# A hybrid decoder step on one core: the 64x64 inversions composed from 16x16 blocks by a block-nilpotent Horner scheme

## What is computed

```python
L = jnp.where(strict, jnp.einsum('nbhcd,nbhsd->nbhcs', k_beta, kb) * decay, 0.0)
eye = jnp.eye(C, dtype=L.dtype)                      # C = 64
tinv = lax.linalg.triangular_solve(eye + L, jnp.broadcast_to(eye, L.shape),
                                   left_side=True, lower=True, unit_diagonal=True)
u = jnp.einsum('nbhcs,nbhse->nbhce', tinv, v_beta)
w = jnp.einsum('nbhcs,nbhsd->nbhcd', tinv, k_beta * jnp.exp(gc)[..., None])
```

## Time and profile before

| | |
|---|---|
| median of three runs | 2028.67 us (2026.51 to 2037.93) |
| span of the profiled execution | 2031.9 us |
| TensorE matmuls busy | 1902.7 us, 94% |
| TensorE weight loads busy | 1734.3 us, 85% |
| VectorE busy | 1255.8 us, 62% |
| ScalarE busy | 938.5 us, 46% |
| mean granted TensorE clock | 0.960 |

### The profile page before, as it was taken

How to read it: one execution, slowest core, us unless ns; L and a number is a source line. 1 busy time by engine, 2 the same in 40 slices (tenths; PEclk the granted TensorE clock), 3 DMA queues, 4 the chain that set the end, 5 groups by cost and what they waited for, 6 DMA issues and landing times.

```text
span 2031.9 us, 45422 instructions
## 1 busy us (share of the span) xinstructions
PE 1902.7 (94%) x19380; PEld 1734.3 (85%) x19380; DVE 1255.8 (62%) x2186; ACT 938.5 (46%) x1834; POOL 77.3 (4%) x158
## 2 busy tenths in 40 slices
PE   5999989989999988889999999899899999889998
PEld 4899978888888777788989999788899788679997
DVE  3545356765446765778556654578654585769953
ACT  3334455544456534423444444645443664353343
POOL 0000000110000100000000000001200011000000
PEclk8999999988999998999999999999899999899999
DMA  8877755555465565699775666545543445269873
GB/s 256 239 225 219 209 164 167 164 148 150 138 167 156 151 157 136 186 269 279 208 203 156 178 178 186 166 135 156 135 122 102 135 120 147 69 160 259 252 201 108
DMA packets 556519, 353.38 MB, mean 174 GB/s; under 512 B 19620, under 2 KB 515270, under 8 KB 555022
## 3 DMA queue, kind: packets, MB, share of 16 engines
q1 hardware_dynamic: 490634, 302.74, 52.3%
q10 hardware_dynamic: 60756, 38.81, 7.2%
q0 software_dynamic: 4928, 8.92, 1.8%
HBM read 332.27 MB, written 18.50 MB: 173 GB/s over the span
## 4 chain that ended last, share of the span: by engine, by line
PE 75%; DVE 10%; DMA 6%; ACT 5%; issue 3%; POOL 1%; SPq 0%; ACTq 0%; DVEq 0%; POOLq 0%
PE bank L926 72%; DMA ring<-in_w_ada 2%; DMA ring<-in_ffn_up 2%; DVE ring_r L744 2%; PE bank L657 1%; DVE far L1999 1%; DMA far<-t_blocks 1%; ACT w_hi_r L736 1%; PE bank L670 1%; POOL far L638 1%; DVE y L1999 1%; DVE big L1999 1%; DVE h L2002 1%; PE bank L665 1%; DMA far<-in_state_gdn_ssm 1%
## 5 line engine op out<-in xcount | busy, mean ns | idle before, releaser
L926 PE MATMUL bank<-big_r,w_hi_r 128*128 128x264 f32 x4160 | 1077.7, 293 | 47.5 <-DVE h_r L2002 25.6
L926 PE MATMUL bank<-big_r,ring_r 128*128 128x264 f32 (+1 forms) x3456 | 994.2, 288 | 0.0
L926 PEld LDWEIGHTS bank<-big_r,w_hi_r 128*128 128x128 f32 x4160 | 748.2, 191 | 109.3 <-issue 86.2
L926 PE MATMUL bank<-h_r,w_hi_r 128*128 128x264 f32 x2752 | 797.1, 290 | 0.0
L744 DVE TENSOR_TENSOR ring_r<-ring,w_hi_r 128x1024 fp32r<-128x1024 f32 (+2 forms) x440 | 523.6, 1195 | 391.3 <-ACT w_hi_r L736 387.3
L926 PEld LDWEIGHTS bank<-big_r,ring_r 128*128 128x128 f32 (+1 forms) x3456 | 662.8, 192 | 1.0
L736 ACT CAST w_hi_r<-ring 128x1024 fp32r<-128x1024 f32 (+2 forms) x440 | 452.0, 1028 | 449.0 <-PE bank L926 201.2
L926 PEld LDWEIGHTS bank<-h_r,w_hi_r 128*128 128x128 f32 x2752 | 530.4, 193 | 1.7 <-issue 0.5
L926 PE MATMUL bank<-ring,c 128*32 128x256 f32 x1152 | 94.5, 409 | 17.0 <-DMA ring<-in_w_ada 14.1
L926 PE MATMUL bank<-big,far 64*64 64x64 f32 (+2 forms) x1440 | 101.8, 251 | 0.0
L926 PEld LDWEIGHTS bank<-big,far 64*64 64x64 f32 (+1 forms) x1440 | 85.1, 137 | 9.2 <-issue 8.8
(11 more groups left out here) (304 smaller groups left out, 1946.1 us busy)
## 6 DMA issues: line engine op xcount, KB each, us to landing
ring<-in_ffn_up SPq DMA_DIRECT2D x176, 512.0 KB, 4.9
ring<-in_w_in SPq DMA_DIRECT2D x148, 512.0 KB, 3.7
ring<-in_w_ada SPq DMA_DIRECT2D x144, 512.0 KB, 4.4
ring<-in_ffn_down SPq DMA_DIRECT2D x64, 512.0 KB, 4.5
far<-in_state_gdn_ssm ACTq DMA_DIRECT2D x28, 512.0 KB, 6.3
ring<-in_ffn_down SPq DMA_DIRECT2D x32, 384.0 KB, 3.5
ring<-in_w_out SPq DMA_DIRECT2D x16, 512.0 KB, 4.7
out_sample_gdn_ssm<-far ACTq DMA_DIRECT2D x16, 512.0 KB, 5.5
```

The source lines that it names most:

```text
L926: return pe.matmul(out, lhsT, rhs, start=start, stop=stop)
```

## The change

The 64x64 inverse is composed in another way. With D the block diagonal of 16x16 blocks, X the negated product of the inverse of D with what lies below the block diagonal (in the transposed layout of the kernel), X is block-nilpotent: its fourth power is zero. The inverse is then a Horner scheme in X applied to the inverse of D: each of three steps multiplies by X and adds the inverse of D.

- Step 0 makes X: one product of 32 matmuls, now with 48 columns, in two banks. VectorE masks it with `below`, in two operations of 128x384.
- Step 1: X by the last 48 columns; VectorE adds in two operations of 128x384. Step 2: X by the last 32 columns; one addition of 128x512. Step 3: X by the last 16 columns; one addition of 128x256, straight into the result. Only the transposed inverse is carried, its partner is no longer updated.
- So a run has four products, with 48, 48, 32 and 16 columns, where it had five with 32. Step 1 no longer has its second product. Steps stay in the same turns, and each still waits for VectorE's result of the step before.
- `settled` copies two pieces, 128x256 and 128x512, where it copied one of 128x512. `clear` zeroes 16 columns of each unit in `x_b` where it zeroed 64 (128x256 for 128x1024).
- The setup builds one mask `below` (one select on GpSimd) in place of two masks in `level` (four selects); the row factors `upper` and their three VectorE operations go.

```diff
-        level = sb("level", 2, 32)
-        upper = sb("upper", 2)
+        below = sb("below", 48)
...
-        def level_cols(v, n, side):
-            return v.rearrange("p u (a h t) -> p u a h t", h=2, t=1 << n)[:, :, :, side, :]
-
-        def unit_cols(v, n, side):
-            return v.rearrange("p (a h t) -> p a h t", h=2, t=1 << n)[:, :, side, :]
-
-        def level_bank(bank, n):
-            return banks[bank][:, :].rearrange("p (u a t) -> p u a t", u=UNITS, t=1 << n)
-
-        def pair_cols(both, n, w, side, u=None):
-
-            cols = "p u (a h t) -> p u a h t" if n == 4 else "p u (h a t) -> p u a h t"
-            v = both[:, :, :, w].rearrange(cols, h=2, t=B16)[:, :, :, side, :]
+        def columns(both, w, first, u=None):
+
+            v = both[:, :, first:C, w]
             return v if u is None else v[:, u]
 
-        INV_PE = 5
-
-        def inv_count(run, s):
-            return INV_PE * run + (1, 2, 4, 5)[s]
+        def half_bank(bank):
+            return banks[bank][:, 0:UNITS // 2 * 48].rearrange("p (u t) -> p u t", t=48)
+
+        def whole_bank(bank, n):
+            return banks[bank][:, 0:UNITS * n].rearrange("p (u t) -> p u t", t=n)
 
...
-                i = act.mul(x_b, bm(ident64[:, :], UNITS), 0.0)
+                i = act.mul(x_b[:, :, 48:C], bm(ident64[:, 0:B16], UNITS), 0.0)
...
-            elif s == 2:
-                pe.wait_ge(inv_t.sem, inv_t.at(2 * run + 1))
-            if s % 2 == 0:
-                for u in range(UNITS):
-                    for hf in HALVES:
-                        i = pe.matmul(banks[2][hf, u * 32:(u + 1) * 32].rearrange("p (a t) -> p a t", t=B16), lt[hf, u, :],
-                                      pair_cols(both[hf], n, 0, 0, u), start=True, stop=True)
-                i.then_inc(inv_pe.sem, inv_pe.one())
-                return
-            pe.wait_ge(inv_x.sem, inv_x.at(2 * run + s // 2 + 1))
-            if n < 5:
-                for u in range(UNITS):
-                    for hf in HALVES:
-                        i = pe.matmul(banks[4][hf, u * 32:(u + 1) * 32].rearrange("p (a t) -> p a t", t=1 << n), both[hf, u, :, 1],
-                                      unit_cols(x_b[hf, u, :], n, 0), start=True, stop=True)
-                i.then_inc(inv_pe.sem, inv_pe.one())
+            else:
+                pe.wait_ge(inv_x.sem, inv_x.at(3 * run + s))
             for u in range(UNITS):
                 for hf in HALVES:
-                    i = pe.matmul(banks[3][hf, u * 32:(u + 1) * 32].rearrange("p (a t) -> p a t", t=B16), x_b[hf, u, :],
-                                  pair_cols(both[hf], n, 1, 1, u), start=True, stop=True)
+                    if s < 2:
+                        out = banks[2 + u // 8][hf, u % 8 * 48:(u % 8 + 1) * 48]
+                        moving = columns(both[hf], 1, B16, u) if s else both[hf, u, 0:48, 0]
+                    else:
+                        n = (32, 16)[s - 2]
+                        out, moving = banks[s][hf, u * n:(u + 1) * n], columns(both[hf], 0, C - n, u)
+                    i = pe.matmul(out, x_b[hf, u, :] if s else lt[hf, u, :], moving, start=True, stop=True)
             i.then_inc(inv_pe.sem, inv_pe.one())
 
         def settled(act, run):
 
             lt, both, x_b = inv_sets[run]
-            act.wait_ge(inv_t.sem, inv_t.at(2 * run + 1))
-            act.wait_ge(inv_x.sem, inv_x.at(2 * run + 2))
-            act.copy(lt[:, :, 0:32].rearrange("p u (a t) -> p u a t", t=B16), pair_cols(both, 5, 1, 0)).then_inc(inv_c.sem, inv_c.one())
+            act.wait_ge(inv_x.sem, inv_x.at(3 * run + 3))
+            act.copy(lt[:, :, 0:B16], both[:, :, 0:B16, 1])
+            act.copy(lt[:, :, B16:48], both[:, :, B16:48, 0]).then_inc(inv_c.sem, inv_c.one())
 
         def invert_dve(dve, run, s):
 
             lt, both, x_b = inv_sets[run]
-            n = 4 + s // 2
-            dve.wait_ge(inv_pe.sem, inv_pe.at(inv_count(run, s)))
-            if s % 2 == 0:
-                by = level[:, n - 4, :].rearrange("p (a t) -> p a t", t=1 << n).unsqueeze(1).to_broadcast([P, UNITS, 32 >> n, 1 << n])
-                dve.tensor_tensor(level_cols(x_b, n, 0), level_bank(2, n), by, ALU.mult).then_inc(inv_x.sem, inv_x.one())
-                dve.wait_ge(inv_x.sem, inv_x.all())
+            dve.wait_ge(inv_pe.sem, inv_pe.at(4 * run + s + 1))
+            if s == 3:
+                dve.tensor_tensor(lt[:, :, 48:C], columns(both, 1, 48), whole_bank(3, B16), ALU.add).then_inc(inv_t.sem, inv_t.one())
+                dve.wait_ge(inv_t.sem, inv_t.all())
                 return
-            if n < 5:
-                t_0 = pair_cols(both, n, 0, 0)
-                dve.tensor_tensor(t_0, t_0, level_bank(4, n), ALU.add)
-                dve.wait_ge(inv_pe.sem, inv_pe.at(inv_count(run, s) + 1))
-            tt_1 = pair_cols(both, n, 1, 1)
-            into = lt[:, :, 32:64].rearrange("p u (a t) -> p u a t", t=B16) if n == 5 else tt_1
-            dve.scalar_tensor_tensor(into, level_bank(3, 4), upper[:, n - 4:n - 3], tt_1, ALU.mult, ALU.add).then_inc(inv_t.sem, inv_t.one())
-            dve.wait_ge(inv_t.sem, inv_t.all())
+            if s == 2:
+                i = dve.tensor_tensor(columns(both, 0, 32), columns(both, 1, 32), whole_bank(2, 32), ALU.add)
+            for g in range(2 if s < 2 else 0):
+                us = slice(UNITS // 2 * g, UNITS // 2 * (g + 1))
+                if s == 0:
+                    i = dve.tensor_tensor(x_b[:, us, 0:48], half_bank(2 + g), bm(below[:, :], UNITS // 2), ALU.mult)
+                else:
+                    i = dve.tensor_tensor(both[:, us, B16:C, 0], both[:, us, B16:C, 1], half_bank(2 + g), ALU.add)
+            i.then_inc(inv_x.sem, inv_x.one())
+            dve.wait_ge(inv_x.sem, inv_x.all())
...
-                for n in range(2):
-                    b = 16 << n
-                    v = level[0:64, n, :].rearrange("p (a t) -> p a t", t=b)
-                    select(v, [[-2 * b, 32 // b], [0, b]], -b, 1, ALU.is_ge, 0.0)
-                    select(v, [[2 * b, 32 // b], [0, b]], 2 * b - 1, -1, ALU.is_ge, 0.0)
-                pool.memset(level[64:128, 0, 0:1], -1.0).then_inc(pool_done.sem, pool_done.one())
+                select(below[0:64, :].rearrange("p (a t) -> p a t", t=B16), [[-B16, 3], [0, B16]], -B16, 1, ALU.is_ge, 0.0)
+                pool.memset(below[64:128, 0:1], -1.0).then_inc(pool_done.sem, pool_done.one())
...
-                                pe.wait_ge(inv_t.sem, inv_t.at(4))
+                                pe.wait_ge(inv_t.sem, inv_t.at(2))
...
-                    pe.wait_ge(inv_t.sem, inv_t.at(6))
+                    pe.wait_ge(inv_t.sem, inv_t.at(3))
...
-                        dve.tensor_reduce(upper[:, :], level[:, :, :], AX_X, ALU.add).then_inc(dve_chain.sem, dve_chain.one())
-                        dve.wait_ge(dve_chain.sem, dve_chain.all())
-                        for n in range(2):
-                            i = dve.tensor_scalar(upper[:, n:n + 1], upper[:, n:n + 1], 0.5 ** (4 + n), 1.0, ALU.mult, ALU.add)
-                        i.then_inc(dve_chain.sem, dve_chain.one())
-                        dve.wait_ge(dve_chain.sem, dve_chain.all())
```

More of the change, by code:

```diff
@@ L775, in _ @@
                 pool.memset(mean_all[:, :], 1.0 / D).then_inc(pool_done.sem, pool_done.one())
-                for buf, value in ((ones_all[:, :], 1.0), (ones_half[:, :], 0.0), (masks[:, :, :], 1.0), (level[:, :, :], -1.0)):
+                for buf, value in ((ones_all[:, :], 1.0), (ones_half[:, :], 0.0), (masks[:, :, :], 1.0), (below[:, :], -1.0)):
                     pool.memset(buf, value).then_inc(pool_chain.sem, pool_chain.one())
@@ L1590, in _ @@
                         act.dma_start(masks[64:128, :, :], masks[0:64, :, :]).then_inc(g2_in.sem, g2_in.one())
-                        act.dma_start(level[64:128, :, :], level[0:64, :, :]).then_inc(g2_in.sem, g2_in.one())
+                        act.dma_start(below[64:128, :], below[0:64, :]).then_inc(g2_in.sem, g2_in.one())
                         act.wait_ge(edge_tr.sem, edge_tr.nth(2))
@@ L1870, in _ @@
                                 if run == 1:
-                                    act.wait_ge(inv_t.sem, inv_t.at(2))
+                                    act.wait_ge(inv_t.sem, inv_t.at(1))
                                     act.wait_ge(inv_c.sem, inv_c.at(1))
@@ L1883, in see_state @@
                         act.dma_start(gs_seen[n % 5], sample_state(I["state_gdn_ssm"][l], n)).then_inc(gs_in[n // 2 % 3].sem, gs_in[n // 2 % 3].one())
-                    act.wait_ge(inv_t.sem, inv_t.at(6))
+                    act.wait_ge(inv_t.sem, inv_t.at(3))
                     act.wait_ge(s_pe.sem, s_pe.at(3))
```

## The result

The changed kernel takes 2009.4 us, the median of four runs (2004.23 to 2015.53), against 2033.3 us for the kernel before in the same comparison (2026.51 to 2038.3). The ratio is 0.989 with a 95% interval of 0.9855 to 0.9924, so it is faster by 15 to 29 us, most likely 22. A second set with an unchanged copy gave 0.9875 (0.9843 to 0.9906). The forecast was 2015.8 us and -12.9 us: the sign and the main term held, the size came out too small. The 2009.4 us lie 0.4 us inside the prediction's wide range (2009 to 2022.5) and outside its own (2012 to 2019.5). Part of that is luck: both were worked out from a before of 2028.67 us, and beside after it took 2033.3. The change itself, -22 us, is more than the wide range allowed (2028.67 - 2009 = 19.7 us).

What follows compares the result with a forecast made beforehand. TensorE's instruction stream was taken as the bound, the inversion a small part of it. Terms 11.25 + 0.5 + 0.3 + 0.8 = 12.9 us, from 2028.67 to 2015.8 us; own range 2012 to 2019.5, for 8 in 10 2009 to 2022.5.

Steps and rivals of the forecast that it cites:

- main term: TensorE: one product of 1.94 us fewer in each of six inversion runs, 11.6 us saved.
- wide range: Span of times given 8 chances in 10, reaching into the rivals: 2009 to 2022.5 us.
- The products: TensorE, inversion: weight loads set a product's time, 48 or 16 columns cost as 32; 11.25 us saved after 0.35 given back.
- VectorE in layer 1, run 0: TensorE's wait for VectorE before step 3 grows from 0.31 to about 0.7 us, giving back 0.35 us.
- Rival E: VectorE's queue in run 0 of both layers doesn't move up, losing the removed product there: 9.0 us gain, 2019.7 us; chance 0.12.
- The price of a half-clock stretch: TensorE behind run 0 of layer 0: 10 us at 0.50 costs 4.3 us.
- The clear: ScalarE's clear before run 0 is 0.64 us shorter, TensorE's wait 0.6 us shorter; 0.4 us a layer, 0.8 us.
- Step 3 to run 1: VectorE's lighter step 3 shortens TensorE's wait before run 1 by 0.34 us a layer; counted 0.25 each, 0.5 us.
- rival D: Fewer half-clock stretches, as behind layer 1's run 1: 2.6 us more gain, 5 with part of a second, 2011 us; chance 0.18.
- the prediction's own sign for the clock: Wrong by the clock if stretches at 0.50 after the runs change in number by two or more.
- C: Rival: more half-clock stretches behind TensorE's waits, five of them making it 8.6 us slower, 2037 us; chance 0.05.

Runs made afterwards that it cites:

- e9: Kernel before without step 1's second product and VectorE's addition of it, so its composed inverse lacks that part; 2020.02 us, 0.9928 of before.
- e1: Changed kernel with a fifth product of 32 columns put back in step 1 of each run, its result unread; 2019.76 us, 0.9936 of before.
- e3: Changed kernel with 6 and 4 dense matmuls on constants ahead of TensorE's waits for blocks in runs 0 and 1; 2015.02 us, 0.9903 of before.
- e7: Changed kernel with both the edits of e3 and e4; 2004.58 us, 0.987 of before.
- e6: Changed kernel with the clear of x_b in runs 0 and 2 over all 64 columns again; 2014.12 us, 0.9903 of before.
- e2: Changed kernel with steps 2 and 3 also at 48 columns, the extra ones overwritten, same number of matmuls; 2012.85 us, 0.9897 of before.
- e4: Changed kernel with VectorE's solve of run 1's blocks one turn later; 2010.36 us, 0.9908 of before.
- e5: Changed kernel with that solve, runs 0 and 1 and the clear of run 1 one turn later; 2011.51 us, 0.9897 of before.

## Why the prediction was right, and where it wasn't

**The products: right.** The step "6 x 1.94 = 11.6 us" is what the runs show: 384 records fewer, 2.00 and 1.98 us a product, 13.7 us gained by removing it alone (e9, at the same clock), 11.8 us lost by putting it back (e1). Measured alike, 48 columns cost 0.01 us more than 32 (2.00 for 1.99), inside the stated bound of 0.1 for each. The 67.9 us that the prediction says the old products hold are durations of overlapping records; thirty products at 1.94 us are 58.

**VectorE in layer 1, run 0: the mechanism right, the size wrong.** I expected a wait of about 0.7 us before step 3. The trace has 3.01 us before step 2 and 0.77 before step 3. TensorE's timeline in layer 1, then VectorE's, then the chain of waits:

```profile
1433.78 2.07 PE L652 MATMUL bank<-far 64*64 64x48 f32 x64 [3.23 <-DMA far<-t_blocks]
...
1439.79 1.74 PE L652 MATMUL bank<-far 64*64 64x48 f32 x54
...
1447.65 2.21 PE L652 MATMUL bank<-far 64*64 64x32 f32 x64 [3.01 <-DVE far L677]
...
1455.08 2.04 PE L652 MATMUL bank<-far 64*64 64x16 f32 x64 [0.77 <-DVE far L671]
```

```profile
1440.70 0.38 DVE L602 TENSOR_SCALAR big<-big 128x256 f32<-128x256 f32 x1 [3.78 <-DMA big<-lt_blocks]
...
1446.58 1.01 DVE L677 TENSOR_TENSOR far<-far,bank 128x384 f32<-128x384 f32 x2
...
1457.64 0.41 DVE L667 TENSOR_TENSOR far<-far,bank 128x256 f32<-128x256 f32 x1
```

```profile
1436.52 4.06 DMA big<-lt_blocks
...
1446.66 0.94 DVE far L677 x2
...
1458.09 1.93 ACT far L617
1460.30 3.91 POOL far L628 x7
1464.21 4.57 DMA far<-t_blocks
1468.82 2.80 PE bank L652 x64
```

The order is: VectorE stands 3.78 us at 1440.70 before the fetched blocks of run 1, solves them, and only then adds step 1 of run 0, although TensorE was done with that product at about 1439.79 + 1.74 = 1441.53. Behind it are run 0's last step, the clear of run 1, its scatter and its first product. This chain from a fetch to the products of run 1 runs beside TensorE's dense work, and what TensorE gains ahead of its end becomes idle time later. That the solve in this place is the cause is shown by e3 and e7, which differ by the solve's turn alone and both have the full clock in run 0: 7.0 us of these waits with the solve here, none with it a turn later. Nor are the new operations on VectorE the cause: e9, with the old ones, waited 1.89 and 0.76 us at the same two places, also at full clock. Here the clock had not fallen behind run 0's wait:

```profile
440.00:449.00 9.00, 8.92 (x88) 8.83 (x89) 4.27 (x17) 1.24 (x2) 0.57 (x1) 0.50 0.19 47
...
1434.00:1440.00 6.00, 6.00 (x114) 5.39 (x112) 1.02 (x2) 0.78 (x3) 0.57 (x1) 1.00 0.52 139
```

These two windows of after are run 0 of layer 0 and of layer 1, at 0.50 and 1.00. From 1440 to 1457 us of before, TensorE gained 4.2 us in layer 1, the missing product and a stretch that had been at half clock; by 1465 us it had given 5.2 back, 3.8 of them in the two waits and the rest in a stretch at 0.50 behind the first (1449.6 to 1452.6 us). So over run 0 it was 1.0 us behind where it had been. In the copy, whose run 0 stood at half clock in layer 1 as before's did, 3.0 us were gained by 1457 and 1.4 given back, so 1.7 us were left. Rival E had the mechanism and the place right, then: in after the product's time was lost there, together with a half-clock stretch's. How much is lost differs between executions of the same code. e3 confirms it from the other side.

**The price of a half-clock stretch: too high.** The step "4.3 us for 10 us at 0.50" is the price on TensorE alone. Over the executions it is 0.34 us for one, not 0.43. In run 0 most of it is hidden under the chain above: from run 0's first product to that of run 1, after needs 35.5 us in layer 0 at half clock and the copy 34.1 at full, but in layer 1 after needs 35.0 at full and the copy 33.8 at half. Behind layer 0's loop it is full (4.3 us for 10.2).

**The clear: wrong in what follows from it.** TensorE's wait before run 0 was to be 0.6 us shorter than 2.98; it is 3.43 us in after, 3.12 in the copy, and its product started at 440.08 where it had started at 440.15. The clear itself did shrink as forecast, from 1.07 to 0.43 us, and the scatter behind it started sooner. What took the gain back is the landing of the last block. These are the chain of waits in before, then in after:

```profile
435.88 4.22 DMA far<-t_blocks
```

```profile
430.32 0.43 ACT far L619
...
434.94 5.09 DMA far<-t_blocks
```

The prediction carried the 0.64 us straight through to TensorE's start; the landing varies by more than that from one place to the next (5.32 us in layer 1 of before, where TensorE waited 4.08 us; 3.23 in after). In layer 1 e9, with the long clear, waited 3.15 us, as short as after. So no run shows a wait that the clear made shorter, and the effect on the time (e6) stays unplaced.

**Step 3 to run 1: not contradicted.** TensorE's wait before run 1 went from 3.27 us (L657 at 478.37 in the trace of before) to 2.74 in layer 0, and from 1.89 to 1.75 in layer 1: 0.52 and 0.14 us, where 0.34 was forecast for each. The unchanged kernel had 2.85 us in layer 0 in its second profile, so 0.4 us there are noise.

**The forecast's error is rival D.** It was 12.9 us forecast against 23.6 us of mean span. At equal clock 17.3 ± 1.3 came, so 4 us more than the terms; e6 would give them to the clear, but by no wait that a trace shows, so this part stays open. The other 6.4 us come from 18.8 us less half clock. D had this at 2.6 to 5 us, and by 2009.4 us its 2011 was the nearer number. The stretch that D named, behind run 1 of layer 1, went from 6.8 us at 0.50 in before to 3.4 in after and to none in the copy. By the prediction's own sign for the clock, a change by two or more such stretches, the case is on the edge: the first product of a run met the half clock (it took over 2.1 us) in four runs of before and three of its second profile, in three of after and one of the copy; and the copy's mean clock of 0.972 is outside 0.955 to 0.967.

Where the half-clock time went can be said in part: over runs 0 and 1 of both layers, the three profiles with the old steps (before, its second one, e9) have 31 to 38 us of half clock, the five with the new steps and the turns unchanged (after, the copy, e1, e2, e6) 14 to 31 us, by the mean 34 and 23. So about 11 of the 18.8 us lie there, though single profiles of one code differ by 10. By e9 (155.4 us of half clock) against after (137.3), not the missing product but the rest of the change lowers it. What in the rest does, I don't know: e2 and e4 (136), e3 (132), e5 (137), e6 (139.5) and e1 (144) all keep most of the lowering, so neither columns, nor the clear, nor the turn of the solve is what does it. What they share and e9 lacks is VectorE's work on steps 0 and 1 in halves, the lighter step 3, the second copy in `settled` and the new setup; none of these was tried alone, and the cause stays open. C didn't happen.

## What to carry to other kernels

Count products of small tiles by their weight loads, not by their columns, and check the count by leaving one out of the old kernel: that gave a term clean of the clock. A wait that the trace puts before an engine is worth its length only if no chain of other engines ends behind it at the same time: filling it with work (e3), or moving the run a turn later (e5), moved the idle time to the next wait; filling it and moving the chain's own step too (e7) did not. Where a set of DMAs issued one behind the other on one queue ends a wait, split it over two queues, and look for what stands behind the second one.

## What the hardware showed that was not expected

- The same code gave spans of 2013.8 and 1999.2 us at mean clocks of 0.964 and 0.972. One of the differences, the stretch behind layer 0's loop (28.4 and 23.7 us, at 0.82 and 1.00), starts 13 us behind the last product of run 2.
- An idle time of 3.43 us before run 0 of layer 0 was followed by 0.50; one of 3.12 us at the same place in the copy was not. In the copy, TensorE paid for it with waits for VectorE:

```profile
440.63 2.07 PE L652 MATMUL bank<-far 64*64 64x48 f32 x64 [3.12 <-DMA far<-t_blocks]
...
453.17 2.06 PE L652 MATMUL bank<-far 64*64 64x32 f32 x64 [1.22 <-DVE far L677]
...
460.62 2.04 PE L652 MATMUL bank<-far 64*64 64x16 f32 x64 [1.71 <-DVE far L671]
```

- Four small DMAs took GpSimd's queue 2.26 us to issue and ScalarE's 2.04 us, so in this size the two queues cost nearly the same. What helps is to use both at once: all eight were issued within 2.5 us, where GpSimd's queue alone took 4.47 us in after.
